# One layer of a hybrid transformer: modulation on two column groups, rotary turn on GpSimd, half of the second key's one-hots on GpSimd

## Chip, cores and metric

The kernel runs on one core of one Trainium2 chip. The time is device microseconds from start to end of one execution. A core has TensorE (PE, its weight loads PEld), VectorE (DVE), ScalarE (ACT), GpSimd (POOL) and SyncE (SP), which here issues all loads.

## What is computed

256 tokens of 1024 features pass a mixer (windowed attention, a gated delta rule in both directions, two gates) and a feed-forward net that picks 16 of 16384 experts per head; a second layer follows. All is float32. Three pieces matter here. The first is the modulation before the mixer, for the tokens x and the context tokens ctx:

```python
mod = silu(c) @ w_ada + b_ada            # c: one row for x, one (c_ctx) for ctx; its first 2048 columns: shift, scale
h = rmsnorm(x, norm_mix) * (1 + scale) + shift
p = h @ w_in                             # 39 tiles of 128 columns
```

The second is the rotary turn of queries and keys, `out = v * cos + swapped(v) * sin`, where swapped exchanges halves of 16 features. The third belongs to the experts: expert = 128 * i1 + i2, so the gate of each token is the outer product of a one-hot row of i1, scaled by the gate, and a one-hot row of i2, summed over 128 (head, choice) pairs; this gives the table W (token, i1, i2).

## The kernel before

One program for each engine, written out by hand in order; the engines meet only through counting semaphores. Weights stream through a ring of four tiles of 512 KB (`ring`, 128 x 1024): SyncE loads tile n when tile n - 4 is used up. Each product of a projection is done in three passes on a high and a low part: ScalarE copies the high part of a half tile (`in_hi`), VectorE subtracts to get the low part (`in_lo`), into `w_parts`, a ring of four half tiles, so two tiles ahead; the features are split the same way (`hp_hi`, `hp_lo`).

**Head (L368 to L503, L1197 to L1300, L1876 to L1947).** SyncE issues cols (726 columns of 128 x 4 bytes, 363 KB), mats (449 KB), four modulation tiles, then x and ctx together (2048 KB). 16 modulation tiles in four blocks of 512 columns are multiplied with a stationary matrix of two columns (`csT`, L461); ScalarE evicts a block as two rows (`mod_out`, L1207) and TensorE turns it into columns (L469). After the third block's products TensorE sums the squares of x (L452), ScalarE takes the root (L1211), VectorE the reciprocal (L1892) and the normalisation (L1889), all of x and half of ctx; then it waits for all 16 turned columns (`mod_cols`, L1897 to L1899). It then scales each chunk k of 128 features (`modulate`, L1925) and splits it (L1921), first the 8 chunks of x (c = 0), and between tiles 2 to 4 those of ctx (c = 1). Projection tiles 0 to 3 take x alone (256 columns), tile 4 both.

**Turn (L515, L1974 to L1976).** After tile 18, five products with a permutation matrix (`swap`) go into two banks between tiles 19 and 20; VectorE multiplies and adds (`rope`, 15 operations of 256 elements), and the third and later products wait for it. The scores (L526) of the attention follow after tile 21. Before that, in tiles 7 to 18, VectorE does twelve convolutions (`conv`, L1958, L1960), five operations each.

**Delta rule.** Products of the level inversion post `y_done`, the turns beside them `z_turned`.

**W stage (L930 to L950, L1533 to L1540, L2416 to L2436).** 32 groups of 8 tokens, two buffers. VectorE compares `iota` with the first keys of seven tokens (`hot1`, L2419), gates the finished group before last (`w_gate`, L2414), compares the second keys of eight tokens (`hot2`, L2423), and makes the eighth token's `hot1` with its gate in one operation (L2426). ScalarE scales the seven with the gates (L1536) and evicts the previous group (L1530). TensorE multiplies one token after the other (L947), eight to a group, and does one or two of the 64 plain expert products before each group (L930). GpSimd has nothing to do in this stage.

## Time and profile before

| | us |
|---|---|
| median of 3 runs (lowest, highest) | 1754.86 (1754.44, 1756.94) |
| the profiled execution | 1755.32 |
| its span | 1753.5 |
| TensorE busy in it | 1691.8 (96%) |
| VectorE busy | 1309.0 (75%) |
| ScalarE busy | 1071.8 (61%) |
| GpSimd busy | 161.9 (9%) |

Busy time is the union of an engine's instructions. The profiled execution is one of its own and lies within the spread of the runs. TensorE is busy nearly everywhere, so what moves the end is where it waits, or where another engine paces it; an average over the span doesn't show that, a table of a stretch or a timeline does. "Idle before <- X" names what ended an idle time. Matmul records come in two per float32 product.

### The profile page before, as it was taken

To read this page: it belongs to the slowest core of one execution; us is meant where nothing else is said; L and a number is where in the kernel's file an instruction comes from. 1 tells how busy PE (TensorE), PEld (TensorE's weight loads), DVE (VectorE), ACT (ScalarE), POOL (GpSimd) and SP (SyncE) were. 2 spreads that over 40 slices of the span, in tenths; PEclk is the share of its full clock that TensorE was granted. 3 is DMA by queue.
4 is the path that set the end of the run, shared out by engine and by line. 5 is a ranking of instruction groups with operands and counts; after the bars stand their busy time and mean duration, and the time that the engine had idled before them with its cause. 6 is when DMAs were issued, how large, how long until landed. Compare 5 with 4: busy or idle time off the path is not lost.

```text
span 1753.5 us, 34071 instructions
## 1 busy us (share of the span) xinstructions
PE 1691.8 (96%) x11462; PEld 1518.8 (87%) x11462; DVE 1309.0 (75%) x2642; ACT 1071.8 (61%) x2218; POOL 161.9 (9%) x136
## 2 busy tenths in 40 slices
PE   7998998999999999999999999999899999999998
PEld 1887688989999878888899999999799898999997
DVE  3788787668989798667666666666776777878887
ACT  2545566735666698666555555555558666666665
POOL 0000005501737200000000000000010000010000
PEclk9899999999999999999999999999999999999999
DMA  8534542125455411555555555555364544555553
GB/s 300 184 106 145 183 150 73 54 97 193 161 175 179 144 37 49 191 192 191 192 185 186 191 183 188 184 187 191 114 214 142 180 139 139 181 181 186 186 183 128
DMA packets 77271, 283.33 MB, mean 162 GB/s; under 512 B 8576, under 2 KB 8576, under 8 KB 76928
## 3 DMA queue, kind: packets, MB, share of 16 engines
q1 hardware_dynamic: 77184, 282.19, 48.5%
q8 instruction: 52, 0.85, 0.2%
q14 instruction: 35, 0.29, 0.1%
HBM read 281.11 MB, written 1.05 MB: 161 GB/s over the span
## 4 chain that ended last, share of the span: by engine, by line
PE 78%; DVE 12%; ACT 5%; issue 2%; POOL 1%; DMA 1%; PEld 0%; PEldq 0%; SPq 0%; ACTq 0%; POOLq 0%; DVEq 0%
PE banks L905 20%; PE banks L893 17%; PE banks L984 9%; PE banks L1145 7%; PE banks L496 6%; PE banks L1169 3%; PE banks L835 2%; DVE split L2423 2%; PE banks L461 2%; DVE arena L2419 2%; PE banks L998 1%; PE banks L684 1%; DMA arena<-wstream 1%; PE banks L1105 1%; PE banks L669 1%
## 5 line engine op out<-in xcount | busy, mean ns | idle before, releaser
L1503 ACT ACTIVATE split<-arena 128x512 fp32r<-128x512 f32 x492 | 309.0, 629 | 134.9 <-PE banks L893 76.9
L893 PEld LDWEIGHTS banks<-split 128*128 128x128 f32 x2880 | 355.4, 192 | 10.5 <-DVE split L2349 3.1
L905 PE MATMUL banks<-split 128*128 128x512 f32 x1536 | 361.9, 390 | 1.0 <-issue 1.0
L893 PE MATMUL banks<-split 128*128 128x256 f32 x2880 | 358.8, 283 | 3.1 <-DVE split L2349 2.3
L2441 DVE TENSOR_TENSOR split<-arena,split 128x512 fp32r<-128x512 f32 x396 | 270.5, 690 | 105.4 <-ACT split L1503 99.7
L905 PEld LDWEIGHTS banks<-split 128*128 128x128 f32 x1536 | 283.8, 188 | 57.3 <-issue 1.4
L1481 ACT ACTIVATE split<-arena 128x512 fp32r<-128x512 f32 x312 | 194.5, 628 | 109.9 <-PE banks L1145 52.8
L984 PE MATMUL banks<-split 128*128 128x256 f32 x1728 | 216.6, 286 | 4.3 <-DVE split L2519 3.9
L984 PEld LDWEIGHTS banks<-split 128*128 128x128 f32 x1728 | 211.8, 193 | 7.2 <-issue 6.0
L2496 DVE TENSOR_TENSOR split<-arena,split 128x512 fp32r<-128x512 f32 x180 | 123.0, 695 | 59.5 <-ACT split L1481 57.6
L496 PE MATMUL banks<-split 128*128 128x256 f32 (+1 forms) x912 | 147.1, 320 | 4.3 <-DVE split L1915 3.4
L496 PEld LDWEIGHTS banks<-split 128*128 128x128 f32 x912 | 131.0, 195 | 23.0 <-issue 10.6
L1145 PEld LDWEIGHTS banks<-split 128*128 128x128 f32 x1056 | 129.7, 192 | 2.3 <-DVE split L2762 0.7
L1145 PE MATMUL banks<-split 128*128 128x256 f32 x1056 | 130.8, 283 | 0.5 <-DVE split L2762 0.5
L2935 POOL TENSOR_TENSOR arena<-arena 128x256 f32<-128x256 f32 x12 | 11.5, 957 | 1018.5 <-ACT arena L1653 678.5
L2757 DVE TENSOR_TENSOR split<-arena,split 128x512 fp32r<-128x512 f32 x128 | 87.1, 692 | 14.5 <-ACT split L1481 14.5
L2947 POOL TENSOR_TENSOR split<-arena,split 128x512 fp32r<-128x512 f32 x68 | 90.8, 1360 | 58.7 <-DVE split L2349 51.2
L2451 DVE TENSOR_TENSOR arena<-arena 128x256 f32<-128x256 f32 x80 | 49.1, 613 | 40.4 <-ACT arena L1552 40.3
L947 PEld LDWEIGHTS banks<-split,arena 128*128 128x128 f32 x512 | 59.6, 191 | 17.0 <-DVE split L2423 16.8
L1536 ACT ACTIVATE arena<-arena 128x128 f32<-128x128 f32 x224 | 69.0, 388 | 7.3 <-DVE arena L2419 4.8
L1218 ACT ACTIVATE split<-arena 128x512 fp32r<-128x512 f32 x78 | 48.1, 624 | 36.8 <-PE banks L496 25.5
L1915 DVE TENSOR_TENSOR split<-arena,split 128x512 fp32r<-128x512 f32 x76 | 50.9, 688 | 26.0 <-ACT split L1218 25.3
(425 smaller groups left out, 2342.2 us busy)
## 6 DMA issues: line engine op xcount, KB each, us to landing
arena<-wstream SPq DMA_DIRECT2D x525, 512.0 KB, 3.3
arena<-x_t SPq DMA_DIRECT2D x1, 2048.0 KB, 12.9
arena<-matsa SPq DMA_DIRECT2D x1, 1260.5 KB, 6.2
out_t<-arena SPq DMA_DIRECT2D x4, 256.0 KB, 2.0
arena<-mats SPq DMA_DIRECT2D x1, 576.0 KB, 8.0
arena<-crow SPq DMA_DIRECT2D x1, 512.0 KB, 7.1
arena<-rows SPq DMA_DIRECT2D x1, 512.0 KB, 5.9
arena<-mats SPq DMA_DIRECT2D x1, 449.0 KB, 3.8
```

What stands on the lines that cost most here:

```text
L496: mm = pe.matmul(ps[:, b, 0:m], w_parts[:, c, (2 * t + k // 4) % 4, P * (k % 4):P * (k % 4) + P], hp[:, e, k, 0:m], start=(k == 0 and c + ...
L893: mm = pe.matmul(ps[:, 4 + b, 0:S], w_parts[:, c, (2 * m + half) % 4, P * k:P * k + P], h_parts[:, e, 4 * half + k, :], start=(half == 0 a ...
L905: mm = pe.matmul(ps[:, 2 * tt + half, :], g_parts[:, e, j % 2, P * tt:P * tt + P], w_parts[:, c, (2 * m + half) % 4, :], start=(first and ...
L984: mm = pe.matmul(out, w_parts[:, c, (2 * m + half) % 4, P * k:P * k + P], src[:, e, 4 * half + k, :], start=(half == 0 and k == 0 and c + ...
L1145: mm = pe.matmul(ps[:, 4 + 2 * (f % 2) + m, 0:S], w_parts[:, c, (2 * (M_FFN + x) + half) % 4, P * k:P * k + P], ff_parts[:, e, 4 * half + ...
L1481: act.activation(w_parts[:, 0, h % 4, :], ring[:, slot, 512 * half:512 * half + 512], ACT.Copy).then_inc(sem["w_hi"], 1)
L1503: act.activation(w_parts[:, 0, (2 * m + half) % 4, :], ring[:, peer_slot(m), 512 * half:512 * half + 512], ACT.Copy).then_inc(sem["w_hi"], 1)
L1536: act.activation(hot1[g % 2][:, t, :], hot1[g % 2][:, t, :], ACT.Identity, scale=rT[:, 2, 8 * g + t:8 * g + t + 1]).then_inc(sem["hot1_sca ...
L2441: dve.tensor_tensor(w_parts[:, 1, (2 * m + half) % 4, :], ring[:, slot, 512 * half:512 * half + 512], w_parts[:, 0, (2 * m + half) % 4, :] ...
L2496: dve.tensor_tensor(w_parts[:, 1, h % 4, :], ring[:, tile_of(M_IN2 + t) % RING, 512 * half:512 * half + 512], w_parts[:, 0, h % 4, :].bitc ...
L2757: dve.tensor_tensor(w_parts[:, 1, h % 4, :], ring[:, tile_of(M_FFN + x) % RING, 512 * half:512 * half + 512], w_parts[:, 0, h % 4, :].bitc ...
L2947: pool.tensor_tensor(w_parts[:, 1, (2 * m + half) % 4, :], ring[:, (N_PEER + m) % RING, 512 * half:512 * half + 512], w_parts[:, 0, (2 * m ...
```

## The change

The modulation's stationary matrix `csT` is padded with zeros to 32 columns, and the two products of a tile go to output rows 0 to 31 and 32 to 63, that is to two column groups of the array; a product with a selecting matrix `sel` adds the two and turns them. The blocks are taken in the order 0, 2, 1, 3, so that shift and scale of the first four feature chunks are complete after two of them (`mod_columns(0)`), and the chunks of x and ctx are scaled in two halves. The sum of squares stands after the first block, all of x and ctx is normalised before the first columns. x is loaded second; cols and mats are cut in two, and the later part, matsa, crow and mats1 are loaded between projection tiles. The five permutation products stand behind tiles 12 to 16, ScalarE evicts them (`swap_out`), and GpSimd does the turn; scores(0) and scores(1) stand behind tiles 19 and 20. In the delta rule z_turned is merged into y_done. In the W stage ScalarE scales six tokens instead of seven, VectorE makes two gated ones, and the second keys' one-hots are made by GpSimd for tokens 0 to 3 and by VectorE for 4 to 7. The diff, cut (left out: the merging of z_turned, renamed counts, column offsets, the host's layout):

```diff
+MOD_BLOCKS = (0, 2, 1, 3)
+part_at = lambda c, k: KT * (k // 4) + 4 * c + k % 4 + 1
...
-MATS = dict(ident=128, ones=128, iota=128, alibi=512, eps=1, eps2=1)
+EARLY_COLS, EARLY_MATS = 132, 260
+
...
-            sp.dma_start(colbuf, cols_in).then_inc(sem["params_in"], 16)
-            sp.dma_start(mats, mats_in).then_inc(sem["params_in"], 16)
+            sp.dma_start(colbuf[:, 0:EARLY_COLS], cols_in[:, 0:EARLY_COLS]).then_inc(sem["params_in"], 16)
+            sp.dma_start(xc.rearrange("p c k t -> p (c k t)"), x_t).then_inc(sem["x_in"], 16)
+            sp.dma_start(mats[:, 0:EARLY_MATS], mats_in[:, 0:EARLY_MATS]).then_inc(sem["x_in"], 16)
             for n in range(RING):
                 sp.dma_start(tile_at(n), wstream[n]).then_inc(loaded[n], 16)
-            sp.dma_start(xc.rearrange("p c k t -> p (c k t)"), x_t).then_inc(sem["x_in"], 16)
...
-            load_freed_by_splits(N_WIN + RING, N_WIN + 3 * RING)
+            load_freed_by_splits(N_WIN + RING, N_WIN + 9)
             sp.dma_start(matsa, matsa_in).then_inc(sem["late_in"], 16)
+            load_freed_by_splits(N_WIN + 9, N_WIN + 11)
+            sp.dma_start(colbuf[:, EARLY_COLS:], cols_in[:, EARLY_COLS:]).then_inc(sem["late_in"], 16)
+            sp.dma_start(mats[:, EARLY_MATS:], mats_in[:, EARLY_MATS:]).then_inc(sem["late_in"], 16)
             sp.dma_start(crow, crow_in).then_inc(sem["late_in"], 16)
+            load_freed_by_splits(N_WIN + 11, N_WIN + 12)
             sp.dma_start(mats1, mats1_in).then_inc(sem["late_in"], 16)
-            load_freed_by_splits(N_WIN + 3 * RING, N_ADA2 + EARLY_TAILS + RING)
+            load_freed_by_splits(N_WIN + 12, N_ADA2 + EARLY_TAILS + RING)
             load_freed_by_matmuls(N_ADA2 + EARLY_TAILS + RING, N_OUT + RING)
...
-            pe.wait_ge(sem["silu_c"], 1)
-            for i in range(2):
-                for half in range(2):
-                    pe.wait_ge(sem["mod_bank_free"], 2 * i + half + 1)
-                    for q in range(4):
-                        pe.wait_ge(loaded[q], 32 * i + 16 * half + 16)
-                        for k in range(2):
-                            mm = pe.matmul(ps[0:2, half, :], csT[:, 2 * q + k, :], ring[:, q, 512 * k:512 * k + 512],
-                                           start=(q == 0 and k == 0), stop=(q == 3 and k == 1))
-                        mm.then_inc(sem["tiles_done"], 1)
-                    if i and half == 0:
-                        sum_squares(0, 512)
-                for half in range(2):
-                    pe.wait_ge(sem["mod_bank_free"], 2 * i + half + 3)
-                    for t in range(8 * i + 4 * half, 8 * i + 4 * half + 4):
-                        mm = pe.transpose(ps[:, 2, 2 * t:2 * t + 2], modrow[0:2, P * t:P * t + P], ident[0:2, 0:2])
-            mm.then_inc(sem["mod_cols"], 1)
+            def mod_products(j):
+
+                pe.wait_ge(sem["mod_bank_free"], j + 1)
+                for q in range(4):
+                    tile_ready(4 * j + q)
+                    for k in range(2):
+                        mm = pe.matmul(ps[32 * k:32 * k + 32, j % 2, :], csT[:, 2 * q + k, :], tile_at(4 * j + q)[:, 512 * k:512 * k + 512],
+                                       start=(q == 0), stop=(q == 3))
+                    mm.then_inc(sem["tiles_done"], 1)
+
+            def turn_mod(j):
+
+                pe.wait_ge(sem["mod_bank_free"], j + 3)
+                for t in range(4 * MOD_BLOCKS[j], 4 * MOD_BLOCKS[j] + 4):
+                    mm = pe.matmul(ps[:, 2, 2 * t:2 * t + 2], modrow[0:64, P * t:P * t + P], mat("sel")[0:64, :], start=True, stop=True)
+                if j % 2:
+                    mm.then_inc(sem["mod_cols"], 1)
+
+            pe.wait_ge(sem["silu_c"], 2)
+            mod_products(0)
+            sum_squares(0, 512)
+            mod_products(1)
+            turn_mod(0)
+            turn_mod(1)
+            mod_products(2)
+            mod_products(3)
+            turn_mod(2)
+            turn_mod(3)
 
...
                 in_tile(t)
                 if t == 6:
                     turn_columns(5, 0)
-            pe.wait_ge(sem["late_in"], 48)
-            swap(0)
-            swap(1)
+                if t == 12:
+                    pe.wait_ge(sem["late_in"], 80)
+                if 12 <= t < 17:
+                    swap(t - 12)
             in_tile(19)
-            swap(2)
-            swap(3)
+            scores(0)
             in_tile(20)
-            swap(4)
             turn_columns(18, 3)
+            scores(1)
             in_tile(21)
-            scores(0)
-            scores(1)
             in_tile(22)
             scores(2)
...
-                for t in (7, 0, 1, 2, 3, 4, 5, 6):
-                    if t == 7:
-                        pe.wait_ge(sem["hot1_gated"], g + 1)
+                for t in (6, 7, 0, 1, 2, 3, 4, 5):
+                    if t >= 6:
+                        pe.wait_ge(sem["hot1_gated"], 2 * g + t - 5)
                     else:
-                        pe.wait_ge(sem["hot1_scaled"], 7 * g + t + 1)
+                        pe.wait_ge(sem["hot1_scaled"], 6 * g + t + 1)
...
+            def mod_out(j):
+                act.wait_ge(sem["tiles_done"], 4 * j + 4)
+                b = MOD_BLOCKS[j]
+                act.activation(modrow[0:64, 512 * b:512 * b + 512], ps[0:64, j % 2, :], ACT.Copy).then_inc(sem["mod_bank_free"], 1)
...
-            mod_out(0)
-            mod_out(1)
-            act.activation(small[:, 84:85], eps, ACT.Sqrt)
-            mod_out(2)
-            roots(0, 512)
-            mod_out(3)
-            for h in range(4):
-                in_hi(h // 2, h % 2)
...
-            for k in range(KT):
+            mod_out(0)
+            act.activation(small[:, 84:85], eps, ACT.Sqrt)
+            roots(0, 512)
+            mod_out(1)
+            for c in range(2):
+                for k in range(4):
+                    hp_hi(c, k)
+            mod_out(2)
+            mod_out(3)
+            for half in range(2):
+                in_hi(0, half)
+            for k in range(4, KT):
                 hp_hi(0, k)
+                if k in (4, 6):
+                    in_hi(1, k // 2 - 2)
             in_out(0)
-            for k in range(4):
+            for k in range(4, KT):
                 hp_hi(1, k)
             in_out(1)
-            for k in range(4, 6):
-                hp_hi(1, k)
             in_out(2)
-            for k in range(6, KT):
-                hp_hi(1, k)
+            def swap_out(t):
+                act.wait_ge(sem["swap_done"], t + 1)
+                if t >= 2:
+                    act.wait_ge(sem["roped"], 2 * t - 2)
+                act.activation(swp[:, t % 2, :], ps[:, t % 2, 0:S], ACT.Copy).then_inc(sem["swapped"], 1)
+
             for t in range(3, 20):
                 in_out(t)
-            act.wait_ge(sem["late_in"], 48)
+                if 13 <= t < 18:
+                    swap_out(t - 13)
+            act.wait_ge(sem["late_in"], 80)
             act.activation(crow, crow, ACT.Silu)
...
+            def norm_factor(c):
                 link(dve.reciprocal(rstd[:, S * c:S * c + S], root[:, S * c:S * c + S]))
-                for k in range(KT if c == 0 else 4):
-                    o = normalise(c, k)
-            link(o)
-            dve.wait_ge(sem["mod_cols"], 1)
-            link(dve.tensor_tensor(modT[:, 0:16, :], bank(2, 16, 2), bc(col("b_ada")[:, 0:16], 2, 2), ALU.add))
-            link(dve.tensor_scalar(gain1, modT[:, 8:16, :].rearrange("p a b -> p b a"), 1.0, None, ALU.add))
-            link(dve.tensor_tensor(gain1, gain1, bc(col("norm_mix"), 1, 2), ALU.mult))
+
+            def mod_columns(h):
+
+                cut = lambda v: v.rearrange("p (s k) c -> p s k c", s=2)[:, :, 4 * h:4 * h + 4, :]
+                m = slice(4 * h, 4 * h + 4)
+                dve.wait_ge(sem["mod_cols"], h + 1)
+                link(dve.tensor_tensor(cut(modT[:, 0:16, :]), cut(bank(2, 16, 2)), cut(bc(col("b_ada")[:, 0:16], 2, 2)), ALU.add))
+                link(dve.tensor_scalar(gain1[:, :, m], modT[:, 8 + 4 * h:12 + 4 * h, :].rearrange("p a b -> p b a"), 1.0, None, ALU.add))
+                link(dve.tensor_tensor(gain1[:, :, m], gain1[:, :, m], bc(col("norm_mix")[:, m], 1, 2), ALU.mult))
...
-            def modulate_parts(c, k0, k1):
-                for k in range(k0, k1):
+            def normalise_all(c):
+                norm_factor(c)
+                for k in range(KT):
+                    o = normalise(c, k)
+                link(o)
+
+            def modulate_four(c, k0):
+                for k in range(k0, k0 + 4):
                     modulate(c, k)
-                    if c == 0 and k in (2, 4):
-                        for half in range(2):
-                            in_lo(k // 2 - 1, half)
                     if k > k0:
                         hp_lo(c, k - 1)
-                hp_lo(c, k1 - 1)
-
-            modulate_parts(0, 0, KT)
-            for t, k0, k1 in ((2, 0, 4), (3, 4, 6), (4, 6, KT)):
+                hp_lo(c, k0 + 3)
+
+            def both_halves(t):
                 for half in range(2):
                     in_lo(t, half)
-                if k0 >= 4:
-                    for k in range(k0, k1):
-                        o = normalise(1, k)
-                    link(o)
-                modulate_parts(1, k0, k1)
+
+            normalise_all(0)
+            normalise_all(1)
+            mod_columns(0)
+            modulate_four(0, 0)
+            modulate_four(1, 0)
+            both_halves(0)
+            mod_columns(1)
+            modulate(0, 4)
+            for k in (5, 6, 7):
+                modulate(0, k)
+                hp_lo(0, k - 1)
+                if k < 7:
+                    in_lo(1, k - 5)
+            hp_lo(0, 7)
+            both_halves(2)
+            modulate_four(1, 4)
+            both_halves(3)
+            both_halves(4)
 
             taps = col("conv", 12, 5)
...
-            def rope(t):
-                dve.wait_ge(sem["swap_done"], t + 1)
-                v = qaT[:, t, :] if t < 4 else kaT[:, 0:S]
-                dve.tensor_tensor(v, v, mat("cos"), ALU.mult)
-                link(dve.tensor_tensor(swp[:, t % 2, :], ps[:, t % 2, 0:S], mat("sin"), ALU.mult))
-                dve.tensor_tensor(v, v, swp[:, t % 2, :], ALU.add).then_inc(sem["roped"], 1)
...
-            dve.wait_ge(sem["late_in"], 48)
-            rope(0)
-            rope(1)
+            dve.wait_ge(sem["late_in"], 80)
             both_lo(21)
-            rope(2)
-            rope(3)
+            logits(0, 0)
             both_lo(22)
-            rope(4)
-            logits(0, 0)
             logits(0, 1)
...
-                dve.tensor_tensor(hot1[g % 2][:, 0:7, :], bc(mat("iota"), 1, 7), bc(rT[:, 0, 8 * g:8 * g + 7], 2, P), ALU.is_equal).then_inc(
+                dve.tensor_tensor(hot1[g % 2][:, 0:6, :], bc(mat("iota"), 1, 6), bc(rT[:, 0, 8 * g:8 * g + 6], 2, P), ALU.is_equal).then_inc(
                     sem["hot1_ready"], 1)
                 if g >= 2:
                     w_gate(g - 2)
-                dve.tensor_tensor(hot2[:, g % 2, :, :], bc(mat("iota"), 1, 8), bc(rT[:, 1, 8 * g:8 * g + 8], 2, P), ALU.is_equal).then_inc(
-                    sem["hot2_ready"], 1)
-                t = 8 * g + 7
-                dve.tensor_scalar(hot1[g % 2][:, 7, :], mat("iota"), rT[:, 0, t:t + 1], rT[:, 2, t:t + 1],
-                                  ALU.is_equal, ALU.mult).then_inc(sem["hot1_gated"], 1)
+                dve.tensor_tensor(hot2[:, g % 2, 4:8, :], bc(mat("iota"), 1, 4), bc(rT[:, 1, 8 * g + 4:8 * g + 8], 2, P), ALU.is_equal)
+                for i in (6, 7):
+                    t = 8 * g + i
+                    dve.tensor_scalar(hot1[g % 2][:, i, :], mat("iota"), rT[:, 0, t:t + 1], rT[:, 2, t:t + 1],
+                                      ALU.is_equal, ALU.mult).then_inc(sem["hot1_gated"], 1)
...
+            def rope(t):
+                pool.wait_ge(sem["swapped"], t + 1)
+                v = qaT[:, t, :] if t < 4 else kaT[:, 0:S]
+                pool.tensor_tensor(v, v, mat("cos"), ALU.mult)
+                pool.tensor_tensor(swp[:, t % 2, :], swp[:, t % 2, :], mat("sin"), ALU.mult).then_inc(sem["roped"], 1)
+                pool.wait_ge(sem["roped"], 2 * t + 1)
+                pool.tensor_tensor(v, v, swp[:, t % 2, :], ALU.add).then_inc(sem["roped"], 1)
+
+            for t in range(5):
+                rope(t)
...
+            pool.wait_ge(sem["phase"], 4 * 3)
+            for g in range(S // 8):
+                if g >= 2:
+                    pool.wait_ge(sem["w_psum"], 8 * g - 8)
+                for i in range(4):
+                    t = 8 * g + i
+                    o = pool.tensor_scalar(hot2[:, g % 2, i, :], mat("iota"), rT[:, 1, t:t + 1], None, ALU.is_equal)
+                o.then_inc(sem["hot2_ready"], 1)
```

## Rows read from the trace of the kernel before

**Rows 1.** Table of stretches, 45.5 to 52 us; columns: length; busy and (count) of PE, PEld, DVE, ACT, POOL; granted clock, DMA share, GB/s.
```profile
45.50:52.00 6.50, 5.65 (x23) 5.15 (x24) 6.25 (x16) 2.61 (x6) 0.00 (x0) 0.50 0.51 165
```

**Rows 2.** Timeline, 7 to 43 us; columns: start, length, engine, line, operation, count, idle before.
```profile
7.94 16.98 PE L461 MATMUL banks<-arena 128*2 128x512 f32 x32 [7.94 <-DMA arena<-wstream]
...
20.83 2.63 DVE L1880 TENSOR_TENSOR arena<-arena 128x512 f32<-128x512 f32 x4 [0.35 <-ACT arena L1203]
...
25.57 1.28 ACT L1223 ACT_TABLE_LOAD   x1
...
33.95 7.03 PE L461 MATMUL banks<-arena 128*2 128x512 f32 x16
...
34.06 0.69 ACT L1211 ACTIVATE arena<-banks,arena 128x512 f32<-128x512 f32 x1 [0.47 <-PE banks L452]
...
34.78 1.75 DVE L1892 RECIPROCAL arena<-arena 128x256 f32<-128x256 f32 x1 [11.32 <-ACT arena L1211]
...
39.25 1.75 DVE L1892 RECIPROCAL arena<-arena 128x256 f32<-128x256 f32 x1
...
42.50 0.19 DVE L1897 TENSOR_TENSOR arena<-banks,arena 128x32 f32<-128x32 f32 x1
```

**Rows 3.** The page's DMA issues: the load of x.
```profile
arena<-x_t SPq DMA_DIRECT2D x1, 2048.0 KB, 12.9
```

**Rows 4.** Loads of the first four weight tiles (line L371): issue to landing.
```profile
DMA to landing us min/median/max: 6.1/7.4/8.5
```

**Rows 5.** Timeline, 52 to 58 us: first eviction of a projection tile, four context chunks.
```profile
52.60 0.38 ACT L1254 ACTIVATE arena<-banks 128x256 f32<-128x256 f32 x1 [1.13 <-PE banks L496]
...
54.14 0.73 DVE L1925 TENSOR_SCALAR arena<-arena 128x256 f32<-128x256 f32 x2
...
56.93 0.43 DVE L1921 TENSOR_TENSOR split<-arena,split 128x256 fp32r<-128x256 f32 x1 [0.15 <-ACT split L1231]
```

**Rows 6.** Groups of TensorE instructions, 60 to 420 us: column groups of 64, and full width.
```profile
L546 PE MATMUL banks<-arena 128*64 128x128 f32 x128 | 8.8, 279 | 1.7 <-ACT arena L1315 1.7
...
L699 PE MATMUL banks<-arena 128*128 128x128 f32 x64 | 8.6, 277 | 0.3 <-DVE arena L2207 0.3
```

**Rows 7.** Waits of TensorE, 60 to 170 us: total, times, longest.
```profile
PE banks L515 <- DVE arena L1976: 1.8, 2, 1.4
...
PE banks L526 <- DVE arena L1985: 0.8, 1, 0.8
```

**Rows 8.** Table of stretches, 95 to 125 us, columns as in rows 1.
```profile
95.00:125.00 30.00, 30.00 (x134) 24.86 (x133) 26.18 (x41) 12.70 (x23) 0.00 (x0) 1.00 0.30 98
```

**Rows 9.** Timelines of GpSimd (first row) and VectorE, 420 to 425 us.
```profile
423.49 0.79 POOL L2937 TENSOR_TENSOR arena<-arena 128x256 f32<-128x256 f32 x1
...
420.30 0.69 DVE L2265 TENSOR_TENSOR split<-arena,split 128x512 fp32r<-128x512 f32 x1 [0.35 <-ACT split L1443]
...
423.62 1.22 DVE L2265 TENSOR_TENSOR split<-arena,split 128x512 fp32r<-128x512 f32 x1
```

**Rows 10.** Timeline of VectorE in the W stage, 642 to 645.5 us.
```profile
642.15 0.34 DVE L2426 TENSOR_SCALAR arena<-arena 128x128 f32<-128x128 f32 x1
642.40 1.08 DVE L2419 TENSOR_TENSOR arena<-arena 128x896 f32<-128x896 f32 x1
643.41 0.55 DVE L2414 TENSOR_TENSOR arena<-banks,arena 128x384 f32<-128x384 f32 x1
643.88 1.22 DVE L2423 TENSOR_TENSOR split<-arena 128x1024 fp32r<-128x1024 f32 x1
645.01 0.34 DVE L2426 TENSOR_SCALAR arena<-arena 128x128 f32<-128x128 f32 x1
```

**Rows 11.** Timeline of TensorE in the W stage, 641 to 643 us.
```profile
641.60 1.03 PE L930 MATMUL banks<-arena 128*128 128x256 f32 x4
642.64 2.02 PE L947 MATMUL banks<-split,arena 128*128 128x128 f32 x16
```

**Rows 12.** Timeline of ScalarE in the W stage, 643 us.
```profile
643.52 2.15 ACT L1536 ACTIVATE arena<-arena 128x128 f32<-128x128 f32 x7 [0.16 <-DVE arena L2419]
```

48 lines of the change are left out of this document (24 added, 24 removed).

## Prediction

> **What bounds the kernel now.** I read the page first, then tables of stretches and timelines of three places, because the diff touches three: the first 70 us, the turn of queries and keys near 130 to 150 us, and the stage that builds the gate table W near 598 to 695 us. In each the question is which wait ends last. Elsewhere the diff only renames a semaphore (y_done counts what y_done and z_turned counted), at no cost, since the same matmul posts the same kind of signal to the same waiters.
>
> At the start TensorE runs the modulation products from 7.94 us, 16 matmul records per column block, and 7.03 us a block once its clock is up [rows 2]. Only then come the modulation columns, the scaling by VectorE, and the split into high and low parts. The first projection tile starts at 45.5 us and crawls, one chunk per VectorE step; TensorE had idled, and from 45.5 to 52 us its granted clock is 0.50, the 1.2 GHz level [rows 1]. In the turn of the queries TensorE waits 1.8 us for the turned tiles and 0.8 us for score buffers [rows 7]. In the W stage VectorE is busy without a gap: its five starts in a row are 0.25, 1.01, 0.47 and 1.13 us apart, 2.86 us for a group of eight tokens [rows 10]. ScalarE is nearly as full (seven scalings in 2.15 us, plus one eviction) and waits only 0.16 us [rows 12], TensorE needs 1.04 us for a plain product pair [rows 11] and some 1.9 for its 16 one-hot records, at most 2.9 and on average less, since some groups have one plain product.
>
> **The change, part by part.**
>
> *Head.* The x tensor is loaded second instead of last; only the needed parts of cols and mats come before the tiles. Before, x landed 12.9 us after its issue at 3.56 [rows 3], that is at 16.5. The first tile landed 6.1 us after 1.66 (at 7.8, with 363 + 449 + 512 = 1324 KB sent), the fourth 8.5 us after its issue near 3.1 (11.6) [rows 4]: 1536 KB in 3.8 us, 404 KB/us. Now 66 KB of cols, 2048 of x and 130 of mats go first, 2244 KB: landed at 7.8 + 920/404 = 10.1 us; the four tiles at 11.3, 12.6, 13.9 and 15.2. Squares and their sums end 6.9 us after x (23.46 against 16.5 [rows 2]): at 17.0.
>
> The two matmuls of a tile now go to columns 0 to 31 and 32 to 63 of the array and can overlap. The attention product does the same with two groups of 64: 128 records take 8.8 us, 0.069 each, where full-width ones of the same length take 8.6/64 = 0.134 [rows 6]. So I halve: 3.5 us a block with the clock up, up to 7 while it is low. Block 0 then ends between 16 and 18 (last tile 15.2). ScalarE evicts it (0.6), loads its table and touches it (1.5), and takes the root (0.7) [rows 2]: VectorE can begin at 19.4 to 21.1; I take 20.5, against 34.78.
>
> VectorE then does both halves of the normalisation, 4.47 us each (34.78 to 39.25 [rows 2]): 29.4. The first column half is long there (block 1 near 23). Its columns cost 0.65 (three linked small operations of 0.19 and less [rows 2]), four chunks of either token set 3.22 each (54.14 to 57.36 [rows 5]): 30.1, then 36.5. ScalarE, which stands in the same chunks, evicts blocks 2 and 3 only after them (1.1) and splits tile 0 (1.1): the first projection product starts near 38.5. Second columns, four more chunks and four half tiles in between (0.65 each) end near 45.1, tile 0 near 45.5. Before, its eviction started at 52.60 [rows 5]. The gain is 7.1 us. Tiles 1 to 4 have the same kind of lockstep as before (the remaining chunks of the context, two half tiles per tile), so I carry 7 us through, at the low clock in both: TensorE again idles before tile 0. Loads cost nothing here: matsa, the rest of cols and mats, crow and mats1 stand between tiles 8 and 12, where a tile is wanted only every 2.6 to 5.2 us and the queue is two thirds idle (DMA share 0.30 in rows 8, further on). If TensorE stays low longer, or x lands later by 2 us, the gain is 5; if VectorE meets fewer waits in the chunks, 9.
>
> *Turn of queries and keys.* Five permutation products move behind tiles 12 to 16, ScalarE evicts each, and GpSimd does the 15 tensor operations. The products cost the same on TensorE; their waits (1.8) and the score wait (0.8) go: 2.6 us. What can eat it is VectorE. In this stretch it is busy 26.18 of 30 us [rows 8], nearly all in two-input operations, and such an operation does not run beside GpSimd's: the one issued at 423.62, 0.13 after a GpSimd operation of 0.79, took 1.22 instead of the 0.69 of its fellow at 420.30, so 0.53 late [rows 9]. Fifteen times 0.53 is 8 us, against 3.8 us of slack in those 30. VectorE may end the convolutions 4 us late, but its five turns there (about 6 us) are gone, and the half tiles it makes are two tiles ahead of use. I take 1.7 us of gain, between 2.6 and a loss of 1.5.
> The Trainium skill (SBUF — State Buffer, Who interferes with whom) calls the shared port pair an exclusive lock, taken for the whole instruction by whichever is first. Rows 9 agree. By that rule full GpSimd durations would add 15 x 0.79, 12 us, and cost the whole of this gain.
>
> *W stage.* VectorE loses one token of seven in the first one-hots and four of eight in the second, and gains one single-token operation. By the two lengths (1.13 for 1024, 1.01 for 896 [rows 10]) 128 elements are 0.12 us: 0.89 + 0.47 + 0.65 + 0.50 = 2.51 us per group. ScalarE drops one of seven scalings, 0.3 us. TensorE's own need, 2.6 on average, is then the floor. GpSimd makes four single-token one-hots per group, and every VectorE operation but the gating (0.47) has to take turns with them. The trace has no GpSimd operation of this form; the nearest is the 256-element, two-input one whose blocking was 0.53 [rows 9]. Half the elements and one input make about a quarter, 0.13, if all of it scales; I take 0.17 with something fixed. Four are 0.68, of which the gating hides 0.47: 2.72 us a group, 0.14 less than 2.86, over 31 groups 4.3 us of gain. Ends: no blocking, TensorE's floor, 8 us of gain; full 0.53 each, 2.51 + 2.12 - 0.47 = 4.16, 40 us of loss. That end I don't believe for a quarter of the data; an op at half of it (0.27) gives 3.12, 8 us of loss, and this is where my range stops.
> The Trainium skill (GPSIMD Engine Reference, Elementwise — side-by-side cycle accounting) gives 1.8 cycles an element at best, 769 ns for 512. An estimate from that page is 0.19 us for 128 elements; with it the group comes to 2.80 and the gain to 2 us.
>
> Sum against the profiled run (1755.32 us, span 1753.5): 7.1 + 1.7 + 4.3 = 13.1 us, so 1742.2. The median shown is 0.5 below that run: 1742 rounded.
>
> **Rivals.** *GpSimd sets the W stage.* Each of its operations waits for a VectorE one, and each then holds VectorE back. At 0.27 us each the group is 3.12 and the stage 8 us longer; with 7.1 and 1.7 the sum is still 0.8 faster, no change, 1754. At 0.35 (half the elements of rows 9, both inputs' worth, something fixed) it is 2.51 + 1.40 - 0.47 = 3.44, 18 us longer: 1764, slower. It decides from about 0.3 us each on. For it: VectorE leaves the port free for little but the gating. Against: a quarter of the data.
> *The column groups do not overlap.* A block stays at 7 us and four of them and the sum of squares end at 44; only the order helps. The first half is ready early, the second columns come at 45.7, and tile 0 ends near 51.5; but TensorE has not idled and its clock stays up, which gives some 2 us over tiles 0 to 1. Head gain 3, total 9: 1746. Against it: rows 6.
> *The W stage falls to TensorE's floor.* Blocking is hidden; 8 us there, and up to 9 in the head: 1736.
> *The late convolutions stall TensorE.* VectorE ends 4 to 6 us late, tile 20 waits for its half tiles: 1.5 lost instead of 1.7 won, 1745.
>
> **How the numbers follow.** Forecast, 1742: 0.50. TensorE's floor, 1736: 0.18. No overlap, 1746: 0.06. Late convolutions, 1745: 0.10. GpSimd with blocking near 0.2 to 0.27, 1747 to 1754: 0.09. GpSimd beyond, slower: 0.07. The range 1733 to 1753 leaves out the slower case and some 0.1 at the two ends. A measurement can tell 0.2%, 3.5 us, from no change: faster (below 1751.4) 0.85, within 0.08, slower 0.07.
>
> **What would show it.** After: block products with 3.5 us or the loads' pace in between; the reciprocal at 19 to 21; the first eviction of a projection tile near 45.5; no wait of the permutation products for VectorE; W groups 2.7 us apart, GpSimd's operations near 0.3 each with stretched VectorE ones beside them. I am wrong if the reciprocal starts after 24, if tile 0 ends after 49, if TensorE waits in tiles 17 to 21 for half tiles, or if the one-hot products wait for GpSimd instead of VectorE.

## The result, and the profile after

The changed kernel is slower: 1772.59 us median (1770.03 to 1774.58, 4 runs) against 1755.9 (1754.44 to 1757.38, 4 runs); the ratio is 1.0098, with a 95% interval of 1.0083 to 1.0113, which is 14.6 to 19.8 us. The forecast was 1742, with a range to 1753. The profiled execution of after took 1774.58 us, its span is 1772.8.

The head of the kernel after, from its timeline (start, duration, engine, line, operation, output and inputs):

```profile
9.33 4.28 ACT L1220 ACTIVATE arena<-arena 128x512 f32<-128x512 f32 x8 [6.43 <-DMA arena<-mats]
...
16.72 1.13 PE L459 MATMUL banks<-arena 128*128 128x512 f32 x2
...
19.54 1.75 DVE L1920 RECIPROCAL arena<-arena 128x256 f32<-128x256 f32 x1 [3.28 <-ACT arena L1229]
...
25.35 3.88 PE L467 MATMUL banks<-arena 128*32 128x512 f32 x16
...
38.89 2.34 PE L514 MATMUL banks<-split 128*128 128x256 f32 x12
...
46.46 0.39 ACT L1264 ACTIVATE arena<-banks 128x256 f32<-128x256 f32 x1 [1.11 <-PE banks L514]
```

This is what was hoped for. The squares begin at 9.33 instead of 16.53, the two column groups overlap (16 records in 3.88 us, 0.24 each), and the first projection tile is evicted at 46.46, where [rows 5] had 52.60: 6.1 us earlier. How much of this is the overlap and how much the new order, no run here separates; from the second block on TensorE also waits for its tiles to land (for 1.65 us before its record at 30.88).

The turn of queries and keys, from the same trace: of the waits of TensorE from 60 to 170 us the new one (line waited for, total, times, longest), then GpSimd's three lines (count, shortest, median and longest in ns, first and last start).

```profile
...
PE banks L514 <- DVE split L1945: 0.8, 1, 0.8
L2911 POOL TENSOR_TENSOR arena<-arena x5: 790/936/1286, 103.7 to 127.4; 128x256 f32<-128x256 f32 x5
L2912 POOL TENSOR_TENSOR arena<-arena x5: 1186/1191/1196, 104.5 to 128.3; 128x256 f32<-128x256 f32 x5
L2914 POOL TENSOR_TENSOR arena<-arena x5: 807/1068/1142, 105.8 to 129.6; 128x256 f32<-128x256 f32 x5
```

Both waits of [rows 7] are gone; this one, for a half tile of VectorE (L1945), has come, in the middle of tile 20. VectorE's operations are held by GpSimd's here, those with one tensor input too. One of the two casts and one first operation of a convolution after, and one of the casts before:

```profile
118.11 0.76 DVE L1942 CAST split<-split 128x128 fp32r<-128x128 f32 x1
106.22 0.97 DVE L2004 TENSOR_SCALAR arena<-arena 128x512 f32<-128x512 f32 x1
```

```profile
121.38 0.23 DVE L1912 CAST split<-split 128x128 fp32r<-128x128 f32 x1 [0.59 <-ACT split L1218]
```

L2004 took at most 0.48 us in the kernel before (its line is L1958 there). By the means of these groups of instructions, after (64 to 144 us) against before (70 to 150), VectorE's work grew by some 7 us: the half tiles (L1945) from 688 to 806 ns each, 31 of them, the convolutions by 2.0 us in all, the two casts by 1.1.

A table load of ScalarE behind the scores stands at 145.99 instead of 153.79, 7.8 us earlier, so the turn added some 2 us to the head's 6.

The W stage is where the time went. I measure it from the first large one-hot operation of VectorE to the first down product behind it. Before (first and last starts stand behind the durations):

```profile
L2419 DVE TENSOR_TENSOR arena<-arena x32: 1078/1085/1480, 598.3 to 688.8; 128x896 f32<-128x896 f32 x32
L905 PE MATMUL banks<-split x1536: 387/389/467, 696.6 to 1253.5; 128*128 128x512 f32 x192
```

After, the same two lines, with GpSimd's new one and who waited for it (us, times):

```profile
L2453 DVE TENSOR_TENSOR arena<-arena x32: 947/960/1352, 590.1 to 702.3; 128x768 f32<-128x768 f32 x32
L921 PE MATMUL banks<-split x1536: 387/389/467, 711.4 to 1268.2; 128*128 128x512 f32 x192
L3008 POOL TENSOR_SCALAR split<-arena x128: 594/840/2068, 590.7 to 706.0; 128x128 fp32r<-128x128 f32 x128
...
who waited for it (us, times):
  PEld banks L963: 38.2, 31
  PE banks L963: 25.9, 30
```

The stage took 696.6 - 598.3 = 98.3 us before and 711.4 - 590.1 = 121.3 after: 23.0 us more. TensorE waits for GpSimd in each of 31 groups, and VectorE, which had no gap in [rows 10], now waits for TensorE. The page's group row gives GpSimd's mean, and the chain of waits between 639.5 and 650 us runs through GpSimd alone:

```profile
L3008 POOL TENSOR_SCALAR split<-arena 128x128 fp32r<-128x128 f32 x128 | 114.4, 913 | 1.5 <-PE banks L963 1.5
639.49 10.71 POOL split L3008 x12
```

Twelve operations, three groups, in 10.71 us: 3.57 us a group, where the forecast had 2.72 and before 2.86. One group, operation by operation (timelines of GpSimd and VectorE):

```profile
641.69 1.37 POOL L3008 TENSOR_SCALAR split<-arena 128x128 fp32r<-128x128 f32 x1
643.04 1.09 POOL L3008 TENSOR_SCALAR split<-arena 128x128 fp32r<-128x128 f32 x1
644.11 0.60 POOL L3008 TENSOR_SCALAR split<-arena 128x128 fp32r<-128x128 f32 x1
644.69 0.60 POOL L3008 TENSOR_SCALAR split<-arena 128x128 fp32r<-128x128 f32 x1
...
641.63 0.96 DVE L2453 TENSOR_TENSOR arena<-arena 128x768 f32<-128x768 f32 x1 [0.97 <-PE banks L963]
642.51 0.55 DVE L2448 TENSOR_TENSOR arena<-banks,arena 128x384 f32<-128x384 f32 x1
642.98 0.68 DVE L2457 TENSOR_TENSOR split<-arena 128x512 fp32r<-128x512 f32 x1
643.58 0.65 DVE L2460 TENSOR_SCALAR arena<-arena 128x128 f32<-128x128 f32 x2
```

Two of the four take 0.60, the two that stand beside VectorE's large one-hots (L2453, L2457) take 0.77 and 0.49 more. VectorE's own operations are not stretched.

The sum of the profiled runs: 8 us won before the stage, 23.0 lost in it, and 4.6 more lost behind it, where this execution's granted clock was lower than before's in the same 50 us (window, busy times and counts, clock, DMA share, GB/s); the first fence is after, the second before:

```profile
1400.00:1450.00 50.00, 47.90 (x367) 44.38 (x366) 34.01 (x79) 30.52 (x76) 0.00 (x0) 0.93 0.39 138
```

```profile
1400.00:1450.00 50.00, 50.00 (x438) 47.29 (x437) 36.57 (x87) 33.70 (x91) 0.00 (x0) 1.00 0.44 146
```

The last down product starts at 1268.2 instead of 1253.5, 14.7 us late, which is -8.2 + 23.0 but for rounding; the spans differ by 1772.8 - 1753.5 = 19.3, so 4.6 us came behind it. Whether the change has a part in them is not settled. From the start of the last down product to the end lie 500.0 us before and 500.3 and 499.9 in the two versions below that leave GpSimd out of the stage, 504.6 after, and 499.9 to 504.4 in the eight versions that have it there, six of them 501.6 to 502.3. These are single executions, and the code behind the stage is the same in all.

### The profile page after: what moved, and what is told of

The parts are those of the page before. It is cut to its first block, busy times and chain, and to the rows that moved or that the text cites. A ratio compares the mean times of both kernels' runs of the same rounds, so it can differ in the third digit from the quotient of the medians.

```text
span 1772.8 us, 34246 instructions
## 1 busy us (share of the span) xinstructions
PE 1689.8 (95%) x11478; PEld 1525.7 (86%) x11478; DVE 1302.1 (73%) x2663; ACT 1069.0 (60%) x2191; POOL 291.7 (16%) x279
## 4 chain that ended last, share of the span: by engine, by line
PE 77%; DVE 8%; POOL 7%; ACT 4%; issue 2%; DMA 1%; PEld 0%; PEldq 0%; ACTq 0%; SPq 0%; DVEq 0%
PE banks L921 20%; PE banks L909 17%; PE banks L1000 10%; PE banks L1161 7%; POOL split L3008 6%; PE banks L514 5%; PE banks L1185 3%; PE banks L851 2%; DMA arena<-wstream 1%; PE banks L1014 1%; PE banks L700 1%; PE banks L1121 1%; DVE split L1945 1%; DVE arena L2071 1%; PE banks L685 1%
## 5 line engine op out<-in xcount | busy, mean ns | idle before, releaser
L1530 ACT ACTIVATE split<-arena 128x512 fp32r<-128x512 f32 x492 | 308.9, 629 | 135.0 <-PE banks L909 76.8
L1508 ACT ACTIVATE split<-arena 128x512 fp32r<-128x512 f32 x312 | 194.5, 628 | 111.0 <-PE banks L1161 53.2
L3008 POOL TENSOR_SCALAR split<-arena 128x128 fp32r<-128x128 f32 x128 | 114.4, 913 | 1.5 <-PE banks L963 1.5
L2791 DVE TENSOR_TENSOR split<-arena,split 128x512 fp32r<-128x512 f32 x128 | 87.2, 692 | 14.6 <-ACT split L1508 14.5
L963 PE MATMUL banks<-split,arena 128*128 128x128 f32 x512 | 67.1, 286 | 25.9 <-POOL split L3008 25.9
L1945 DVE TENSOR_TENSOR split<-arena,split 128x512 fp32r<-128x512 f32 x76 | 54.5, 736 | 32.3 <-ACT split L1236 31.9
```

What stands on the lines that cost most here:

```text
L963: pe.matmul(ps[:, 2 * (g % 2) + t // 4, P * (t % 4):P * (t % 4) + P], hot1[g % 2][:, t, :], hot2[:, g % 2, t, :].bitcast(F32), start=True, ...
L1508: act.activation(w_parts[:, 0, h % 4, :], ring[:, slot, 512 * half:512 * half + 512], ACT.Copy).then_inc(sem["w_hi"], 1)
L1530: act.activation(w_parts[:, 0, (2 * m + half) % 4, :], ring[:, peer_slot(m), 512 * half:512 * half + 512], ACT.Copy).then_inc(sem["w_hi"], 1)
L3008: o = pool.tensor_scalar(hot2[:, g % 2, i, :], mat("iota"), rT[:, 1, t:t + 1], None, ALU.is_equal)
```

## The experiments

Each ratio is to the kernel before, measured with it (1756.4 to 1758.1 us). The theories: A, GpSimd's own time per instruction sets the stage; B, its operations are short and wait for VectorE; C, part of the loss lies elsewhere than in the stage.

**The W part undone.** The changed kernel with the W stage of before:

```
-                for i in range(4):
-                    o = pool.tensor_scalar(hot2[:, g % 2, i, :], mat("iota"), rT[:, 1, t:t + 1], None, ALU.is_equal)
+                dve.tensor_tensor(hot2[:, g % 2, :, :], bc(mat("iota"), 1, 8), bc(rT[:, 1, 8 * g:8 * g + 8], 2, P), ALU.is_equal)
```

> The changed kernel with the W stage of the kernel before: VectorE makes all eight second-key one-hots and one gated first-key one-hot, ScalarE scales seven, GpSimd does nothing there; head and rotary turn stay as changed. Theory A (the stage is lost to GpSimd's own time, four operations of about 0.89 us each, 3.57 us a group of eight tokens): the W stage falls from 121.3 us back to about 98.3, and the whole to 1747 or 1748, 8 us under the kernel before (6 from the head, 2 from the turn). Theory C (part of the 17 us is lost elsewhere, in the later stages where TensorE's granted clock dipped to 0.93 between 1400 and 1450 us): the whole stays above 1751, and the dip is still there.

Measured 1749.48 us, ratio 0.995 (0.9931 to 0.9969), 8.8 us under before; the stage is 98.3 us again (591.4 to 689.7). The whole loss, and more, comes with the W part. The whole is 1.5 us above what A expected. C is out as far as it means another part of the change; the few us behind the stage stay open, as said above.

**The W part alone**, on the kernel before (the same edit the other way round).

> The kernel before with the change of the W stage alone. Theory A: the first product behind the stage comes 23 us later than in the kernel before, the groups are 3.57 us apart, GpSimd's operations mean 0.85 to 0.92 us, and the whole is 1778 to 1780. Theory C: the stage costs less here than 23 us, or the whole is longer than the stage explains, above 1782.

Measured 1780.61, ratio 1.013 (1.0113 to 1.0147): 22.9 us, and 0.6 above the 1780 that A allowed. GpSimd's mean is 913 ns again, the stage 601.0 to 720.7, 119.7 us. Head and turn aren't needed for the loss.

**A quarter of the data for GpSimd.**

```
-pool.tensor_scalar(hot2[:, g % 2, i, :], mat("iota"), ...
+pool.tensor_scalar(hot2[:, g % 2, i, 0:32], mat("iota")[:, 0:32], ...
```

> The changed kernel, with each of GpSimd's four operations a group writing 32 elements a partition instead of 128; the other 96 columns of those one-hots are left as they are, so the gate table is incomplete. Theory A with a fixed time per instruction: an operation still takes 0.55 to 0.85 us, since a quarter of the data saves little; the groups are 2.7 to 3.4 us apart and the whole is 1746 to 1768. Theory A with a time that goes with the data (what the prediction assumed when it made a quarter of the time out of a quarter of the data): 0.22 to 0.3 us each, groups 2.6 to 2.7 us apart, 1742 to 1745. Theory B (an operation is short in itself and waits for VectorE's operations to end): the operations that stand beside VectorE's still take 0.5 us and more, while those that fall in its gaps take under 0.2.

Measured 1747.09, ratio 0.994 (0.9924 to 0.9957), stage 96.4 us. The operations, over the stage and one by one:

```profile
L3008 POOL TENSOR_SCALAR split<-arena 128x32 fp32r<-128x32 f32 x128 | 85.6, 714 | 5.0 <-PE banks L963 4.8
L3008 POOL TENSOR_SCALAR split<-arena x128: 353/458/1667, 590.1 to 680.3; 128x32 fp32r<-128x32 f32 x128
```

The mean falls only from 913 to 714 ns for a quarter of the data, the shortest from 594 to 353. So neither the 0.22 to 0.3 of a time that goes with the data, nor one fixed time: 0.35 and 0.6 us when undisturbed, and some 0.3 on top in both on average. A and B both had to be measured apart.

**GpSimd by itself, and beside VectorE.** Two small kernels that compute nothing of the reference.

> A small kernel that leaves out the whole computation: GpSimd runs nine series of eight operations. Series 1 to 7 run with VectorE idle: one-hot of 128 elements into fp32r, into fp32, with a constant instead of a column, a multiplication by a column, the one-hot of 512 elements, products of two tensors of 128 and of 512 elements. Series 8 is the first again beside VectorE's products of two SBUF tensors of 768 elements, series 9 beside VectorE's products with one operand in PSUM, 512 elements. Theory A (own time, mostly fixed): 0.5 to 0.85 us alone for 128 elements, and less than twice that for 512; series 8 and 9 at most 0.2 longer. Theory B (waiting for VectorE): 0.2 to 0.3 us alone, 0.8 and more in series 8, in turns with VectorE, and near 0.3 in series 9. If comparing with a column is what costs, series 3 and 4 are much shorter than 1.

The first, from its timeline; the last four rows are series 8 and 9 with VectorE's operations beside them:

```profile
5.58 4.65 POOL L49 TENSOR_SCALAR r<-v 128x128 fp32r<-128x128 f32 x8 [5.16 <-DMA v<-v_in]
...
24.77 12.32 POOL L53 TENSOR_SCALAR r<-v 128x512 fp32r<-128x512 f32 x8
37.23 3.33 POOL L54 TENSOR_TENSOR a<-v 128x128 f32<-128x128 f32 x8
40.70 9.80 POOL L55 TENSOR_TENSOR a<-v 128x512 f32<-128x512 f32 x8
50.54 7.22 DVE L69 TENSOR_TENSOR w<-v 128x768 f32<-128x768 f32 x8 [48.03 <-POOL a L55]
52.46 8.56 POOL L56 TENSOR_SCALAR r<-v 128x128 fp32r<-128x128 f32 x8 [1.96 <-DVE w L69]
61.06 9.65 DVE L74 TENSOR_TENSOR w<-v,banks 128x512 f32<-128x512 f32 x16 [3.30 <-POOL r L56]
62.44 4.64 POOL L57 TENSOR_SCALAR r<-v 128x128 fp32r<-128x128 f32 x8 [1.41 <-DVE w L74]
```

Undisturbed, the one-hot of 128 elements costs 4.65/8 = 0.58 us from start to start, 0.60 each, and series 2 to 4 (other output type, a constant, a multiplication) took 4.64 to 4.66 as well. 512 elements cost 1.56 each (1561 ns in the group row), so 0.96/384 = 2.5 ns an element and 0.28 us fixed. Beside VectorE's products of two SBUF tensors eight of them take 8.56 us: the first three 1.85 to 2.02 us each, the other five, as VectorE's series ends, 0.59. Beside products with one operand in PSUM the eight take 4.64, as alone. A is right on the 0.6 alone, but wrong on 512 elements (2.6 times the time, where it had less than twice) and on series 8; B is right on the waiting in series 8, and wrong on 0.2 to 0.3 us alone and in series 9. The comparison with a column is not what costs.

> A small kernel that leaves out the whole computation. GpSimd runs series of four operations: 1, a one-hot of 32 elements, VectorE idle; 2 to 5, the one-hot of 128 elements beside back-to-back VectorE operations: one-hots of six tokens (2), gated one-hots of one token with one tensor input (3), the pattern of a group of the W stage (4), gated one-hots in turn with gatings that read PSUM (5); 6, a product of 256 elements beside six-token one-hots; 7, a product of 256 elements beside products of two SBUF tensors; 8, a one-hot of 512 elements alone. If GpSimd is held by VectorE's operations on SBUF and has 0.28 us fixed and 2.5 ns an element of its own: 0.36 in series 1, 1.5 to 2 us in series 2, about 0.9 to 1.2 in series 4, near 0.6 to 0.8 in series 5, and VectorE's operations as long as alone (0.95 for six tokens). If VectorE is held by GpSimd as the prediction had it, GpSimd stays at 0.6 in all series and VectorE's operations stretch by 0.2 us and more. Series 3 tells whether the one-input form holds GpSimd too: then over 1 us, else 0.6.

The second small kernel, its lines in the windows of four series (shortest, median and longest in ns, first and last start): GpSimd and VectorE in series 2, the same in series 3, GpSimd in series 4, VectorE and GpSimd in series 7.

```profile
L49 POOL TENSOR_SCALAR r<-v x4: 1847/1848/2031, 9.1 to 14.7; 128x128 fp32r<-128x128 f32 x4
L87 DVE TENSOR_TENSOR w<-v x10: 945/952/1045, 7.2 to 15.3; 128x768 f32<-128x768 f32 x10
...
L49 POOL TENSOR_SCALAR r<-v x4: 597/597/630, 17.9 to 19.7; 128x128 fp32r<-128x128 f32 x4
L88 DVE TENSOR_SCALAR w<-v x32: 332/334/402, 17.2 to 25.4; 128x128 f32<-128x128 f32 x32
...
L49 POOL TENSOR_SCALAR r<-v x4: 977/1244/1469, 27.3 to 30.7; 128x128 fp32r<-128x128 f32 x4
...
L90 DVE TENSOR_TENSOR w<-v x16: 678/679/1214, 51.8 to 63.0; 128x512 f32<-128x512 f32 x16
L56 POOL TENSOR_TENSOR a<-v x4: 1108/1168/1168, 53.2 to 56.5; 128x256 f32<-128x256 f32 x4
```

Beside back-to-back six-token one-hots of VectorE a GpSimd one-hot takes 1.85 us, the time of two of VectorE's (their pitch is 10.01/11 = 0.91), and VectorE loses at most 0.1. Beside VectorE's one-tensor one-hots, which keep it busy without a gap as well, it stays at 0.60. In the W stage's own pattern it takes 1.0 to 1.5. Series 1 gave 0.363 us for 32 elements, as 0.28 + 32 x 2.5 ns. In series 7, where GpSimd multiplies two tensors, VectorE is held: 1.214 instead of 0.678, 0.54 us, the 0.53 of [rows 9].

**Less of VectorE beside the same GpSimd.**

```
-dve.tensor_tensor(hot1[g % 2][:, 0:6, :], bc(mat("iota"), 1, 6), ...
+dve.tensor_tensor(hot1[g % 2][:, 0:6, 0:32], bc(mat("iota")[:, 0:32], 1, 6), ...
-dve.tensor_tensor(hot2[:, g % 2, 4:8, :], bc(mat("iota"), 1, 4), ...
+dve.tensor_tensor(hot2[:, g % 2, 4:8, 0:32], bc(mat("iota")[:, 0:32], 1, 4), ...
```

> The changed kernel, GpSimd's four operations a group untouched, but VectorE's two large one-hot operations write 32 of 128 columns (the other 96 columns of these ten one-hots are left as they are, so the gate table is incomplete). That takes VectorE's work in SBUF from 2.2 to about 1.1 us a group and leaves GpSimd's instructions as they were. If GpSimd's 0.91 us is 0.6 of its own and 0.31 of waiting for VectorE, it falls to 0.65 to 0.75 us, the groups come to 2.7 to 3.0 us (ScalarE and TensorE near 2.6), and the stage ends 17 to 26 us earlier than in the changed kernel: 1747 to 1756. If 0.91 is all GpSimd's own, nothing moves: 3.57 us a group, 1772 to 1775.

Measured 1738.83 us, ratio 0.9895 (0.9877 to 0.9913), stage 592.4 to 678.9, 86.5 us. GpSimd's instructions are untouched and yet:

```profile
L3008 POOL TENSOR_SCALAR split<-arena x128: 591/597/1068, 592.9 to 672.9; 128x128 fp32r<-128x128 f32 x128
```

The median falls from 840 to 597 ns, the mean to 632. This shows it inside the kernel: the waiting comes from VectorE's two large one-hots. It went 8 us further than I expected, since ScalarE and TensorE need less than the 2.7 us a group that I had set as their floor. TensorE is now the bound: from 610 to 670 us it is busy 60.00 of 60, where it had 46.42 in the changed kernel. The run also takes work from VectorE, so it shows who holds GpSimd, and not what the stage would cost with VectorE's work in full. The groups come to (670.9 - 592.4)/31 = 2.53 us, by VectorE's first and last large one-hot.

**VectorE's second-key one-hots in the one-tensor form.**

```
-dve.tensor_tensor(hot2[:, g % 2, 4:8, :], bc(mat("iota"), 1, 4), bc(rT[...], 2, P), ALU.is_equal)
+for i in range(4, 8):
+    dve.tensor_scalar(hot2[:, g % 2, i, :], mat("iota"), rT[:, 1, 8 * g + i:8 * g + i + 1], None, ALU.is_equal)
```

> The changed kernel, in which VectorE makes its four second-key one-hots by four one-token operations with one tensor input (0.26 us apart, 1.04 in all) instead of one operation with two tensor inputs (0.60). VectorE is busy longer, 2.95 us a group. If only VectorE's operations with two tensors in SBUF hold GpSimd, as in the small kernel, GpSimd is held by the first-key one-hots alone: 0.7 to 0.76 us an operation instead of 0.91, groups of 2.95 to 3.05 us, and the whole at 1751 to 1757, some 18 us under the changed kernel. If any busy VectorE holds GpSimd, the groups are 3.57 us and longer, and the whole is 1772 or more.

Measured 1759.8, ratio 1.0016 (1.0005 to 1.0028), stage 107.8 us: about 14 us under the changed kernel, though VectorE has more to do. That is 3 us above the upper end of what I expected, the groups are (691.0 - 591.3)/31 = 3.22 us apart instead of 2.95 to 3.05, and GpSimd's mean is 820 ns instead of 700 to 760:

```profile
L3009 POOL TENSOR_SCALAR split<-arena 128x128 fp32r<-128x128 f32 x128 | 102.5, 820 | 0.0
...
642.07 0.60 POOL L3009 TENSOR_SCALAR split<-arena 128x128 fp32r<-128x128 f32 x1
643.23 1.06 POOL L3009 TENSOR_SCALAR split<-arena 128x128 fp32r<-128x128 f32 x1
644.27 0.68 POOL L3009 TENSOR_SCALAR split<-arena 128x128 fp32r<-128x128 f32 x1
645.57 1.47 POOL L3009 TENSOR_SCALAR split<-arena 128x128 fp32r<-128x128 f32 x1
...
642.76 1.06 DVE L2453 TENSOR_TENSOR arena<-arena 128x768 f32<-128x768 f32 x1 [0.81 <-PE banks L963]
...
645.62 0.94 DVE L2453 TENSOR_TENSOR arena<-arena 128x768 f32<-128x768 f32 x1
```

The long ones are those beside L2453; one that has just begun when it starts waits it out in full (1.47), one that is half done less (1.06). Beside the one-tensor operations there is up to 0.08 that I had not allowed for, and the large one-hot costs up to 0.87 of waiting instead of the 0.4 to 0.6 in my expectation. The form counts, not whether VectorE is busy: the second theory, 1772 or more, is out.

**Fewer tokens for GpSimd**: two and three of eight instead of four, the rest to VectorE (range(4) becomes range(2) or range(3), hot2[:, g % 2, 4:8, :] starts at 2 or 3).

> The changed kernel with GpSimd making two of the eight second-key one-hots instead of four, VectorE six. If the stage is set by the number of GpSimd's operations (0.9 us each, of which 0.6 is its own and 0.3 is waiting while VectorE works in SBUF), two take 1.8 us and VectorE is the bound again: 0.88 + 0.47 + 0.85 + 0.65 = 2.85 us a group, as in the kernel before, and the whole is 1749 to 1750, as with no GpSimd in the stage. If instead every GpSimd operation also costs VectorE time (the prediction's 0.17 us each), the group is 3.2 us and the whole 1758.

> The same with three tokens for GpSimd and five for VectorE. GpSimd 3 x 0.9 = 2.7 us, VectorE 2.73 us: a group of 2.75 to 2.85 us, the whole 1746.5 to 1749.5. If GpSimd's waiting grows with VectorE's fuller share of the time (0.5 us each and more), 3 x 1.1 = 3.3 us and 1762.

Two tokens: 1748.14, ratio 0.9946 (0.9929 to 0.9962), stage 96.5 us. VectorE is the bound again and doesn't suffer from GpSimd, or the stage would be some 11 us longer. Three: 1757.36, ratio 0.9998 (0.9988 to 1.0009), stage 106.1 us; the first expectation missed and its alternative was near:

```profile
L3008 POOL TENSOR_SCALAR split<-arena 128x128 fp32r<-128x128 f32 x96 | 98.6, 1045 | 1.8 <-PE banks L963 1.8
```

Three at 1.045 are 3.1 us a group. The 0.9 of the changed kernel is no constant: with three tokens VectorE's large operations come more often for each of GpSimd's, and each is held longer. With two it is 1.049 on average, no more than with three, so the waiting doesn't simply grow with VectorE's share; why it stops there was not tested.

**A better split**: seven scalings by ScalarE and one gated one-hot by VectorE as before, GpSimd two tokens; then the same with TensorE taking GpSimd's two tokens last.

> The changed kernel with seven first-key one-hots scaled by ScalarE as before the change, one gated by VectorE, and two of eight second-key one-hots made by GpSimd. VectorE needs 1.01 + 0.47 + 0.85 + 0.26 = 2.59 us, GpSimd 1.8, ScalarE 2.15 + 0.69 = 2.84 less what overlaps, about 2.72: the group is 2.72 us and the whole 1745 to 1746, under both kernels. If ScalarE was already level with VectorE in the kernel before, nothing is gained against the version without GpSimd in the stage: 1749.5.

> The best version so far (seven scalings by ScalarE, two of eight second-key one-hots by GpSimd) with TensorE taking the two tokens of GpSimd last in a group and waiting for them only there, and ScalarE scaling in that order. The version before it waited 2.9 us for GpSimd, in the first groups; those go at most: 1745 to 1747.5, 0.6 to 0.7% under the kernel before. If the groups are bound by ScalarE and VectorE anyway, the same as before: 1747.4.

Measured 1747.38, ratio 0.9937 (0.992 to 0.9955), stage 96.2 us; and 1747.86, 0.9949 (0.9935 to 0.9962), stage 95.0. Both beat both kernels, and both are just above the ranges expected (1746 and 1747.5). Against the version without GpSimd in the stage (0.995) they are 2 to 3 us shorter in the stage and not apart in the whole. Taking the pair late brought nothing that the whole shows.

**The head alone**: rotary turn and W stage as before; the late loads and the merged semaphore of the delta rule stay as changed.

> The kernel before with the head alone changed: the rotary turn is again done by VectorE at its old place, and the W stage is the old one. By the trace of the changed kernel (tile 0 ends 6.1 us earlier, tile 4 5.8) the head is worth 6 us: 1752 beside 1758 for the kernel before. The rest of the 8.6 us of the version without the W part, 2.6, would then be the turn. If the turn is worth nothing, this run is at 1749.5; if it is worth all that TensorE waited there (2.6 us) and more, at 1752 to 1753.

1751.02, ratio 0.9963 (0.9948 to 0.9977): 6.5 us, with 4.0 to 9.1 as its interval. The turn is what is left to the first version's 0.995: 2 us by the ratios, 1.5 by the medians, and not apart from nothing by these intervals. That it gives 2 rests on the traces alone: 5.8 us ahead at tile 4 and 7.8 at the table load, and this run's trace, with the old turn, has the old waits of 1.8 and 0.8 us there, where the changed kernel has one of 0.8.

## Why the prediction was wrong

**Head, forecast -7.1: right.** Measured 6.5, and 6.1 in the trace. The reciprocal at 19.54 (19.4 to 21.1 forecast), the columns 0.6, the projection's start at 38.89 (38.5), tile 0 at 46.46 (45.5). The x tensor came sooner than the 10.1 of the working, but that didn't set the reciprocal: ScalarE evicted block 0 at 16.82, when its products had ended, and then loaded its table (1.28 us) before the root at 18.84. The sum of squares (matmuls at 16.72, 1.13 us) was done by then. The rival without overlap is out: 0.24 us a record.

**Turn, forecast -1.7: right as far as it can be told.** GpSimd's fifteen operations took 0.79 to 1.29 us; VectorE got the convolutions done late by one wait of 0.8 us, and both old waits are gone. The prediction named that wait as a mark of being wrong, and the gain stands all the same. GpSimd's products held VectorE by some 7 us in all, 0.45 each, where the working had 8. By the Trainium skill (SBUF — State Buffer, Who interferes with whom) the cost could have been 12 us of VectorE. Its lock is there: series 7 shows it at 0.54 us for each of GpSimd's products, and the casts wait for GpSimd's product to end. But VectorE had room for most of it (from 95 to 125 us it is busy 27.68 of 30), and it no longer makes the five turns; 0.8 us reached TensorE.

**W stage, forecast -4.3, measured +23: the failed step.** The prediction wrote: "Half the elements and one input make about a quarter, 0.13, if all of it scales; I take 0.17 with something fixed." Two things are wrong in it.

First, it priced how long GpSimd holds VectorE and not how long GpSimd itself takes (only its list of signs has "near 0.3 each"). Its floor for the group was TensorE's 2.6 us and VectorE's 2.51; GpSimd's four operations in a row were no term. Undisturbed they are 4 x 0.58 = 2.3 us, near that floor, since 0.28 of each 0.60 doesn't depend on the data. [rows 9] had a whole operation of 0.79 for 256 elements and two inputs. Scaling it by the data gave 0.2; a bound from above, its full 0.79 four times, 3.16 us a group, was there to be read. It would have made the stage 9 us longer and stretched the range to 1756, no change; the 1772.6 measured would still have been outside, for the second reason. The estimate from the Trainium skill (GPSIMD Engine Reference, Elementwise — side-by-side cycle accounting), 0.19 us for 128 elements, made the same error: it took only the part per element (by 1.8 cycles 1.5 ns each; 2.5 measured for this form) and nothing for the start of each instruction. The runs decide: 0.60.

Second, the direction of the blocking. [rows 9] shows GpSimd holding VectorE, for a product of two tensors, and that is right for that form (0.54 in the small kernel). The one-hot has one tensor and a column, and there VectorE's large one-hots hold GpSimd: 0.77 + 0.49 us a group, and VectorE loses nothing that the group shows. With 4 x 0.58 this is 3.58, the 3.57 measured. The working also let VectorE's one-tensor one-hots take turns with GpSimd's; they don't (0.60). GpSimd's own 2.3 us a group would not have made the stage slower: it is under the 2.86 of before, and with most of the waiting gone (0.63 an operation) the whole is 1738.8, though that run has less work for VectorE too. The Trainium skill's rule of an exclusive lock for whichever comes first (the same section) agrees with the 1.85 us beside VectorE's back-to-back one-hots, but not with VectorE's 0.952 beside them; in this form the lock was one-sided.

**The rivals.** "GpSimd sets the W stage" is what happened, and its mark, one-hot products waiting for GpSimd, came true. Its dearer case, 0.35 us each, came to 3.44 us a group and 1764, not far from the 3.57 measured, but by luck: that sum is VectorE's work and holds of 0.35 on it, and the group is in fact four GpSimd operations of 0.91 with no such holds. It had 0.07. The columns did overlap. The late convolutions came in part: tile 20 waits for a half tile, for 0.8 us where that rival lost 1.5 instead of gaining 1.7. TensorE's floor is there (86.5 us of stage when GpSimd is hardly held), behind the others.

## What to carry to other kernels

When work moves to another engine, first write that engine's own row: count of its instructions a period, times a whole duration of the nearest one, unscaled, as the upper bound. A small operation is mostly its fixed part: cut it by the data only where two sizes in a trace show the slope. And ask of each pair of neighbours who holds whom, by their forms: here VectorE's operations with two tensors in SBUF held GpSimd's one-tensor ones, and GpSimd's products held VectorE's, even a cast. So an engine that is "free" may be free only beside some of its neighbour's operations.
